# The final norm's gain spread in expert 5 instead of expert 30, into 4 KB that are free by then

## The reference

```
h = rmsnorm(x, norm_mix_g);      x = x + hybrid_mixer(h)     # conv and gated linear attention
h = rmsnorm(x, norm_ffn_g);      x = x + moe(h)              # top 4 of 32 experts
out = rmsnorm(x, norm_final_g)                               # x / rms(x) * norm_final_g

expert e:  gu = xb @ w_gate_up[e] + b_gate_up[e]             # 1024 -> 2048
           gate = min(gu[:, :1024], 7);  up = clip(gu[:, 1024:], -7, 7)
           y = ((up + 1) * gate * sigmoid(1.702 * gate)) @ w_down[e] + b_down[e]
```

## Time and profile before

| | us |
|---|---|
| median of the runs | 1025.82 |
| the profiled execution | 1025.74 |
| its span, first to last instruction | 1024.0 |
| PE busy | 999.3 |
| DVE busy | 280.2 |
| ACT busy | 149.8 |

### The profile page before, as it was taken

One profiled execution on the slowest core, in us unless ns is written; L12 is line 12 of the kernel. 1 busy time (PEld: TensorE's weight loads), 2 busy tenths in 40 slices (PEclk: granted clock), 3 DMA queues, 4 the chain that ended last, 5 costly groups with the idle time before them and its releaser, 6 DMA issues.

```text
span 1024.0 us, 12746 instructions
## 1 busy us (share of the span) xinstructions
PE 999.3 (98%) x5032; PEld 413.5 (40%) x5032; DVE 280.2 (27%) x685; ACT 149.8 (15%) x302; POOL 9.7 (1%) x27
## 2 busy tenths in 40 slices
PE   9999999999999999999999999999999999999997
PEld 7799733333333333333333333333333333333334
DVE  2888522222112212222222212221121222122122
ACT  1311211110111111111111111111111111111112
POOL 1010000000000000000000000000000000000000
PEclk9999999999999999999999999999999999999999
DMA  9976999999999999999999999999999999999996
GB/s 378 420 310 255 389 357 427 428 426 435 429 433 430 430 430 431 430 431 434 434 430 433 431 433 430 431 431 431 430 430 430 431 431 434 427 427 428 428 420 254
DMA packets 24662, 423.87 MB, mean 414 GB/s; under 512 B 3000, under 2 KB 3648, under 8 KB 6464
## 3 DMA queue, kind: packets, MB, share of 16 engines
q1 hardware_dynamic: 23616, 421.31, 96.8%
q10 hardware_dynamic: 1024, 2.26, 0.6%
HBM read 422.51 MB, written 1.05 MB: 414 GB/s over the span
## 4 chain that ended last, share of the span: by engine, by line
PE 83%; DMA 15%; issue 1%; ACT 0%; DVE 0%; ACTq 0%; POOL 0%; SPq 0%; PEldq 0%; DVEq 0%; POOLq 0%
PE bank L1811 36%; PE bank L1831 19%; DMA ring<-in_w_expert 14%; PE bank L1470 5%; PE bank L1680 5%; PE y L1874 4%; PE bank L1849 3%; PE y L1621 2%; PE bank L1747 1%; PE bank L1922 1%; PE bank L1462 1%; PE bank L1520 1%; PE bank L1855 1%; DMA ring<-in_w_qk 1%; PE bank L1621 1%
## 5 line engine op out<-in xcount | busy, mean ns | idle before, releaser
L1811 PE MATMUL bank<-ring,x_t 128*64 128x512 f32 x1984 | 447.1, 597 | 0.0
L1811 PEld LDWEIGHTS bank<-ring,x_t 128*64 128x64 f32 x1984 | 133.9, 136 | 263.4 <-issue 259.9
L1831 PE MATMUL bank<-ring,act 128*64 128x512 f32 x960 | 223.1, 596 | 10.5 <-DMA ring<-in_w_expert 10.5
L1326 DVE TENSOR_TENSOR gu_b<-bank,bias_t 128x512 f32<-128x512 f32 x64 | 44.3, 692 | 329.9 <-PE bank L1849 329.9
L1831 PEld LDWEIGHTS bank<-ring,act 128*64 128x64 f32 x960 | 66.3, 137 | 136.8 <-issue 136.7
L793 ACT COPY gu_sb<-bank 128x512 f32<-128x512 f32 x64 | 37.5, 586 | 222.7 <-PE bank L1811 222.7
L1279 DVE TENSOR_TENSOR x_t<-bank,cols 128x512 f32<-128x512 f32 x30 | 20.8, 692 | 165.1 <-PE bank L1747 165.1
L1680 PE MATMUL bank<-x_sb,p_row 128*64 128x512 f32 x256 | 60.6, 593 | 0.0
L1265 DVE TENSOR_SCALAR p_row<-slot,rank,rstd 128x64 f32<-128x64 f32 x62 | 16.6, 312 | 160.7 <-PE bank L1855 160.7
L1874 PE MATMUL y<-z,p_t 64*128 64x512 f32 x240 | 59.6, 615 | 0.0
L797 ACT ACTIVATE act<-gu_b 128x256 f32<-128x256 f32 x62 | 25.8, 417 | 195.3 <-DVE gu_b L1332 195.3
(11 more groups left out here) (273 smaller groups left out, 536.3 us busy)
## 6 DMA issues: line engine op xcount, KB each, us to landing
ring<-in_w_expert SPq DMA_DIRECT2D x66, 4096.0 KB, 34.0
ring<-in_w_expert SPq DMA_DIRECT2D x48, 2048.0 KB, 16.7
ring<-in_w_expert SPq DMA_DIRECT2D x12, 1024.0 KB, 10.2
ring<-in_w_in SPq DMA_DIRECT2D x4, 2048.0 KB, 26.5
ring<-in_w_down_last SPq DMA_DIRECT2D x6, 1024.0 KB, 40.9
ring<-in_w_out SPq DMA_DIRECT2D x2, 2048.0 KB, 25.5
ring<-in_w_expert SPq DMA_DIRECT2D x5, 512.0 KB, 5.3
ring<-in_w_in SPq DMA_DIRECT2D x2, 1024.0 KB, 13.5
```

The costliest lines, as they stand in the source:

```text
L1326: dve.tensor_tensor(gu_b[:, :, :, :], bank[2][:, :].rearrange("p (f a s) -> p a f s", a=2, f=4), bias_t[:, :, 4 * h:4 * h + 4, ds(e, 1)] . ...
L1811: ins = mm(bank[h][a * SLOTS:(a + 1) * SLOTS, :], x_t_of(it)[:, k, :], w[:, kk, a, :], start=k == 0, stop=k == KT - 1)
L1831: ins = mm(bank[0][a * SLOTS:(a + 1) * SLOTS, :], act_of(it)[:, k, :], w[:, kk, a, :], start=k == 0, stop=k == KT - 1)
```

## The change

`broadcast_g` and its two copies move from expert 30 to expert 5, into PE's branch behind `add_rows`, and ACT's load of `g8` from behind expert 5 to behind expert 4. `g_bc` moves out of the ring into the space of small tensors that are done by then (`before`, `chosen`, `hot` and others; the list is written in another order so that these stand together). In expert 30 there was work of PE between the first half and the wait for its copy; in the branch there is none, and the branch ends with a wait for the second copy.

```diff
+        spread_at = 20480 + 1024
+        before_at = spread_at + 2048 + 1024
...
+        g_bc = at("g_bc", [P, D], spread_at)
...
-        g_bc = at("g_bc", [P, D], slot_at(SPARE[0]) + 8192)
@@ ACT @@
             for it in range(LOOP_FROM):
                 evacuate(it, it + 1)
-            act_e.wait_ge(s_pref, 1)
-            act_e.dma_start(g8[:, :], norm_final_g.rearrange("(k p) -> k p", p=P)).then_inc(s_gfin, 16)
+                if it == COUNT_AT:
+                    act_e.wait_ge(s_pref, 1)
+                    act_e.dma_start(g8[:, :], norm_final_g.rearrange("(k p) -> k p", p=P)).then_inc(s_gfin, 16)
@@ DVE, activate @@
                 if isinstance(it, int) and it == FILL_AT:
                     keep_table()
+                    for h in range(2):
+                        dve.wait_ge(s_gb, h + 1)
+                        dve.tensor_copy(g_bc[:, h * HALF:(h + 1) * HALF], bank[3][:, :]).then_inc(s_gbk, 1)
@@ DVE, activate_last_two @@
-                for h in range(2):
-                    dve.wait_ge(s_gb, h + 1)
-                    dve.tensor_copy(g_bc[:, h * HALF:(h + 1) * HALF], bank[3][:, :]).then_inc(s_gbk, 1)
@@ PE, products, in the branch @@
                         add_rows(it.odd)
+                        if it.odd == 1:
+                            pe.wait_ge(s_table, 1)
+                            pe.wait_ge(s_gfin, 16)
+                            broadcast_g(0)
+                            pe.wait_ge(s_gbk, 1)
+                            broadcast_g(1)
+                            pe.wait_ge(s_gbk, 2)
@@ PE, products_last_two @@
                 gate_up(a, 1, range(4))
-                pe.wait_ge(s_ptk, a + 1)
-                pe.wait_ge(s_gfin, 16)
-                broadcast_g(0)
                 gate_up(a, 2, range(0, 2))
-                pe.wait_ge(s_gbk, 1)
-                broadcast_g(1)
                 turn(a, 0)
                 gate_up(a, 2, range(2, 4))
-                pe.wait_ge(s_gbk, 2)
                 gather_next(a)
```

More of the change, by code:

```diff
@@ L201, in build @@
         act, gu_b = row((("act", [P, F // P, SLOTS], f32), ("gu_b", [P, 2, 4, SLOTS], f32)), 16384, 20480)
-        (p_t, bdn, gates_t, bias_t, ident, ones, before, slot1, gates, rank1, chosen, table,
+        (p_t, bdn, gates_t, before, chosen, lmax, four, hot, bias_t, ident, ones, slot1, gates, rank1, table,
          cols, ss, ss3, rest, root, var, lnv, rstd, tmp2, eps_c, one_c, n_items, cnt, more, block_c, boff_c, exp_c, place, extra1,
-         hot, n_f, lmax, four, ngt, ssh, minus_half) = row((
+         n_f, ngt, ssh, minus_half) = row((
              ("p_t", [P, T], f32), ("bdn", [P, HALF], f32), ("gates_t", [P, TT, P], f32),
-             ("bias_t", [P, 2, F // P, E], f32), ("ident", [P, P], f32),
-             ("ones", [P, P], f32), ("before", [P, P], f32), ("slot1", [P, P], f32), ("gates", [P, TT, E], f32),
-             ("rank1", [P, TT, E], f32), ("chosen", [P, TT, E], f32), ("table", [1, 2 * TABLE], i32),
+             ("before", [P, P], f32), ("chosen", [P, TT, E], f32), ("lmax", [P, TT, 8], f32), ("four", [P, TT, 8], f32),
+             ("hot", [E, BLOCKS - 1, EXTRA], f32), ("bias_t", [P, 2, F // P, E], f32), ("ident", [P, P], f32),
+             ("ones", [P, P], f32), ("slot1", [P, P], f32), ("gates", [P, TT, E], f32),
+             ("rank1", [P, TT, E], f32), ("table", [1, 2 * TABLE], i32),
              ("cols", [P, NCOLS], f32), ("ss", [P, TT], f32),
@@ L214, in build @@
              ("exp_c", [E, 1], f32), ("place", [E, BLOCKS - 1], f32), ("extra1", [E, EXTRA], f32),
[L215 to L218, removed]
+             ("n_f", [1, BLOCKS - 1], f32), ("ngt", [P, TT], f32), ("ssh", [P, 2, TT], f32), ("minus_half", [P, 1], f32)), 20480, KEPT)
+        spread_at = 20480 + 1024
+        before_at = spread_at + 2048 + 1024
+        bias_at = before_at + 512 + 256 + 2 * 64 + 192
+        gates_at = bias_at + 2048 + 3 * 512
+        table_at = gates_at + 2 * 256
+        assert spread_at + 4 * D <= bias_at
+        g_bc = at("g_bc", [P, D], spread_at)
         g8 = at("g8", [KT, P], before_at)
         table_f = at("table_f", [1, 2 * TABLE], table_at)
-        br_bc = at("br_bc", [P, E], before_at + 2 * 512)
+        br_bc = at("br_bc", [P, E], gates_at)
         h2 = at("h2", [P, TT, KT, P], 16384)
         wr_g, parts_sb, ident4 = row((
-            ("wr_g", [P, KT, E], f32), ("parts_sb", [P, P], f32), ("ident4", [P, E], f32)), 24576, 26624)
+            ("wr_g", [P, KT, E], f32), ("parts_sb", [P, P], f32), ("ident4", [P, E], f32)), bias_at, bias_at + 2048)
         lg, left, ex = row((("lg", [P, TT, E], f32), ("left", [P, TT, E], f32), ("ex", [P, TT, E], f32)), 18432, 20480)
```

## The result

The changed kernel takes 1029.59 us (median of 8 runs, 1028.37 to 1032.16), the kernel before 1025.76 us in the same series (8 runs, 1024.73 to 1026.59). The ratio is 1.0042 (95% interval 1.0033 to 1.0051): 3.8 us or 0.37% by the medians, slower, where no change was forecast (1026.3, range to 1028.2). It went the way of rival B.

What follows compares the result with a forecast made beforehand. The prediction took the weight loads, not PE, to bound the kernel. From 1025.74 us it added 1.2 lost in the stream, subtracted 0.7 gained in expert 30, giving 1026.2, or 1026.3 as median; range 1024.4 to 1028.2.

Steps and rivals of the forecast that it cites:

- rival B: Loads issued from 286 us on: the stream stands still for PE's whole hold, up to 4.1 us, net +3.4, 1029.2; chance 0.09.
- The bound of the kernel: From 222 to 960 us transfers never stop; the last pieces' landing plus a short tail sets the end.
- Expert 30 gives 0.7 us of its 2.16: Expert 30: PE loses 2.16 us of work, 0.7 is gained, the remaining 1.4 to 1.5 become waits for pieces.
- C: Kernel end: the last pieces do not bind and the stream loses nothing, so all 2.16 us stay, 1023.7; chance 0.04.
- The gains land in time, the table is ready: Expert 5: table ready at 277.05, gains at 272.4 with 6 us to spare, before PE arrives at 278.25.
- Sum: 4.1 us for which PE is held: Expert 5: two halves of 1.98 us each and some 0.1 for the branch wait hold PE for 4.1 us.
- the next load issued at about 290.4: Behind expert 5: the load issued at 286.3 before should be issued at about 290.4.
- I take 1.2 us ... so I count the loss once: Loads behind expert 5: the first, with 2.0 us queued, loses 1.2 us; those behind find 3.2 us queued and add nothing.
- a loss of more than 2.7 us: Load stream: losing more than 2.7 us would show the prediction wrong and count as slower.
- A: Loads behind expert 5: 2.0 us of queue is enough, the stream doesn't stop, 0.7 us gained stay, 1025.1; chance 0.24.
- first-byte latency of about 0.6 us: Transfers issued by SP or ACT: by this figure 2.0 us of queue would be ample and the stream lose nothing.
- D: PE's longer loop body: each of 12 passes fetches instructions anew, 64 us, of which 6.4 are hidden, about 1083; chance 0.02.

Runs made afterwards that it cites:

- none: The changed kernel without spreading the gains anywhere; DVE fills g_bc with one constant in expert 5: 1025.11 us against 1025.96 for the kernel before.
- both: The changed kernel with the gains spread a second time, in expert 30 as before: 1030.47 us against 1025.96 for the kernel before.
- busy: The changed kernel with 7 and 8 useless small products in PE's two waits for DVE's copies: 1029.70 us against 1025.91 for the kernel before.
- nostall: The changed kernel with the two halves through PSUM banks 2 and 3, so PE need not wait for the copies: 1026.66 us against 1025.96 before.
- deep: The changed kernel with the gains spread in expert 17 instead of 5, with the same waits: 1025.30 us against 1025.91 for the kernel before.
- busy3: The changed kernel with 3 useless small products in each of PE's two waits for DVE's copies: 1028.59 us against 1025.82 for the kernel before.
- deep_nostall: The changed kernel with the gains spread in expert 17 and over two PSUM banks: 1025.37 us against 1025.82 for the kernel before.
- half: The changed kernel spreading only the first half in expert 5, without PE's wait; the second half is a constant: 1025.45 us against 1025.91 before.
- layout: The kernel before with only the changed kernel's addresses for small tensors and g_bc, gains still spread in expert 30: 1025.92 us against 1025.96.

## Why the prediction was wrong

- **The bound of the kernel: right.** The loads set the end. A hold of PE in expert 17 costs nothing, one in expert 5 costs what the loads lose.
- **Expert 30 gives 0.7 us of its 2.16: right.** Measured 0.85 in the run none (0.7 by its profiled execution), with 1.2 us of new waits; the 0.7 between both and the changed kernel agrees, but is known only to 1.5 us. C, with all of it, is excluded.
- **The gains land in time, the table is ready: right.** PE goes on into the first products without a wait.
- **"Sum: 4.1 us for which PE is held": mis-sized, 5.5 us.** The 4.1 us to the restart are right to the digit. What the sum left out is that PE, with 1.15 us of work in 2.90, came back at half its clock, and 8 matmuls took 1.4 us more. The forecast's sign, the next load issued at about 290.4, came true by luck (290.3): this execution stood 1.4 us earlier at the branch, and the hold was 1.4 us longer.
- **"I take 1.2 us ... so I count the loss once": this is the step that failed.** The loads lost 4.6 us, in three steps of 2.2, 1.9 and 0.5. Two things were wrong in it. With 5.5 us of hold the queue at the first load was 0.2 us deep and not 2.0. And the step took it that, after one loss, a queue of 3.2 us would do for the loads behind, though its own row had lost 1.5 us at 2.4, and none between 2.4 and 6.1 had been seen. Put together, the loads of 4096 KB give the curve: queued 0.2 us, lost 2.2; 2.6, lost 1.9; 3.5, lost 1.3; 4.1, lost 0.5; 4.3, lost 0.2 (the third load of busy); 4.6 and more, lost less than 0.1. Until the queue is back at some 4.5 us, every load loses again. So the total is not a property of the first load: it is the hold less what the queue can spare. Without the hold the first load would have found 0.2 + 5.5 = 5.7 us; less 4.5, that is 1.2 us to spare. This estimate gives 0 for a hold of 1.1 (measured 0), 1.0 for 2.15 (measured 1.3), 4.3 for 5.5 (measured 4.6) and 4.7 for 5.9 (measured 4.8). With the forecast's own hold of 4.1 it would have been 2.9, and the time 1028.0. Of the 3.4 us by which the loss was forecast too small, 1.7 come from this step and the rest from the longer hold. The sign that the prediction gave for being wrong, a loss of more than 2.7 us, stands in the loads.
- **Rival B named the mechanism and the price's order** (three more loads that may each lose; +3.4 against +3.8 measured), and was given 0.09. Its chance followed from the loss counted once. That its price comes so near is in part chance: it took a hold of 4.1 us to be lost whole, and measured were 5.5 us of which 4.6 were lost.
- **A fell** with the loads of nostall: 3.5 us of queue are not enough. With it falls what the prediction worked out from the Trainium skill's first-byte latency of about 0.6 us (DMA: Bandwidth & Descriptors, section Specifications). The figure itself is not far off here: after the issue at 290.35 the first packets of that load start at 291.3, 1.0 us later. It is no measure of the queue that is needed. **D fell:** from 222 to 960 us the changed kernel, too, moves only two instruction packets, and deep has one more branch in each pass and shows no loss.

The profiled executions close the account. The changed kernel's loads stood 1.9 us earlier than those of before (the load issued ahead of the branch lands at 290.5, against 292.4), and lost 4.6: from 334 us to 1001 us each of them lands 2.6 to 2.7 us later than in before, so nothing of the loss is made good. PE's end gave back 0.8: together +1.9. The 1.9 us at the start are no part of the change: in the twelve profiled executions this landing lies between 290.5 and 293.6. The span grew by 3.5. The other 1.6 us lie in one landing, at 1005.0 us where 1003.5 was due, which PE waited 2.1 us for and not 0.5 as in none. That landing isn't part of the change: see the last section.

## What to carry to other kernels

Work that is moved in a kernel bound by its loads costs nothing only where the queue of loads is deep; read at the new place how much is queued when the next load is issued (the landing before, less the issue), and compare the whole hold with what exceeds some 4.5 us of it (for loads of this size), not with the whole queue. A loss recurs until the queue has recovered, so work out the end of the chain and not its first step. Look also at what the waiting engine's clock does behind the gap, and let products and copies overlap over two banks before moving them: that took 3.1 of the 3.8 us away here.

## What the hardware showed that I had not expected

- A queue of transfers loses time long before it is empty: with 4.1 us still to land 0.5 us went, with 3.5 us 1.3, with 4.6 us and more nothing. The packets show part of the reason. Each load has 16 packets under 512 B, as many as there are engines; I read them as each engine's sign that its share is done. For the load that lands at 292.4 in the kernel before, 10 of the 16 stand between 289.0 and 290.2 (the first at 289.2, 3.2 us ahead of the landing):

```profile
DMA packets 26, 0.52 MB, mean 437 GB/s; under 512 B 10, under 2 KB 10, under 8 KB 10
```

So the first engine has done its share 3.2 us before the load has landed. In the changed kernel, where the next load was not ready, the 16 signs of the load that lands at 290.5 stand between 288.2 and 290.1. No packet starts from 290.1 to 291.3, and the first 16 behind that (291.3 to 291.9) take 301.8% of 16 engines over 0.6 us, or 1.8 us each, where they otherwise take 1.2:

```profile
DMA packets 0, 0.00 MB, mean 0 GB/s; under 512 B 0, under 2 KB 0, under 8 KB 0
```

```profile
q1 hardware_dynamic: 16, 0.52, 301.8%
```

3.2 us, and the 1.0 from issue to first packet, add up to 4.2: an estimate of the depth that is needed, near the 4.1 to 4.6 where the loss ends. It isn't the whole account. Behind the hole the engines end together (all 16 signs between 301.5 and 302.2, of the load that lands at 302.4), and the load issued at 299.8 loses 1.9 us even so; why is open.

```profile
DMA packets 22, 0.20 MB, mean 281 GB/s; under 512 B 16, under 2 KB 16, under 8 KB 16
```

- PE's clock fell to half behind 4.1 us in which it was busy for 2.3, as well as behind 4.1 us filled with small products (busy3), but not behind 5.9 us with more of them (busy). Behind the 2.15 us of two banks it stayed full in nostall and fell in deep_nostall, where PE was busy throughout.
- Loads of 2048 KB ran at 428 GB/s and of 4096 KB at 431.
- Single landings near the end (970 to 1005 us) come late, in some executions and not in others: by 1.5 us in the profiled execution of the changed kernel (at 1005.0 us, 1 MB 4.0 us after the landing ahead of it, by issue and time to landing, and 2.5 before), by 1.5 us in those of nostall and busy3, and by 0.3 to 0.7 us in those of both, half and layout (the instructions of layout there are those of before). The other six have none. The cause was not found. It may be behind the wider spread of the changed kernel's runs (3.8 us against 1.9), which stays open.
